# Two top-k retrievals: candidate pairs summed on GpSimd instead of VectorE, ten row steps and several orders moved

## The chip, the cores and the metric

One Trainium2 chip, of which the kernel uses one core. The metric is the device time of one execution in microseconds. Engines are called as in the profile: PE (TensorE), PEld (its weight loads), DVE (VectorE), ACT (ScalarE), POOL (GpSimd) and SP (SyncE).

## The reference

One step of a hybrid decoder layer over 1024 prompt tokens and 64 sample tokens, model width 1024: dilated sliding-window attention, a gated width-3 convolution, a merge, a layer norm, then PEER, a product-key expert layer, and a second norm. What matters here is the retrieval in PEER, for each token and each of 8 heads:

```python
s1 = einsum('chk,nk->chn', qy[..., :half], k1)      # 128 scores, side 0
s2 = einsum('chk,nk->chn', qy[..., half:], k2)      # 128 scores, side 1
v1, i1 = lax.top_k(s1, 16)
v2, i2 = lax.top_k(s2, 16)
cand = v1[..., :, None] + v2[..., None, :]           # pairs of candidates
cid = i1[..., :, None] * 128 + i2[..., None, :]
sc, pos = lax.top_k(cand, 16)
eid = take_along_axis(cid, pos)                      # 16 of 16384 experts
g = softmax(sc)
out = sum_k (g * gelu(x . u[eid])) * v[eid]
```

## The kernel before

Tokens are in two halves: EARLY (A, 512 tokens, four tiles of 128) and LATE (B, 576 tokens, five tiles, the last with 64). The stages follow one another, each a block that all engines leave together: attention; convolution gates, branches, norm and retrieval of A; the same four stages of B; `build_gates`; `experts`; the second norm.

The two halves use different expert paths. For B, `build_gates` makes a dense gate matrix and `experts` multiplies all 16384 experts on PE. For A, each of 512 (token tile, choice) pairs is a *row*: POOL fetches the chosen rows of u and v by indirect DMA (`fetch_rows`), DVE takes a dot product (`dot_row`), ACT a Gelu per eight rows (`row_gelus`), and DVE adds the weighted v row (`weigh_row`). One `row_step(y)` is the dot of row y and the weighted sum of row y-16. The 528 row steps are laid by hand into the stages of B: 60 into the convolution, 16 into the branches, none into norm, retrieval and gates, 452 into `experts`. Inside a stage, `spread(y0, total, weights)` lays them on slots; the convolution has 40 slots (8 output tiles, five units each: unit 1 carries the taps, unit 2 the gated product) with equal weights. u rows and v rows have rings of four buffers, so POOL fetches row y+4 when `dotted` says that row y is done.

In a retrieval, for each head and side x: PE makes queries (`split3`, three matmuls for full precision), ACT copies their high part (`q_hi`), POOL subtracts to get the remainder (`q_lo`), PE makes scores, ACT copies them (`s_copied`). POOL also makes the weight remainder of the next head (`split_w`, `w_lo`). DVE ranks each side (`top16`: max, match_replace, max, two max_index), adds candidate pairs (`cand`, 16x4 + 12x4 of them per token), converts indices to f32 (`ixf`), chooses the best 16 pairs and splits their positions (`pos_ready`). POOL then turns positions into a distance to 0..15 (L1534, L1921), ACT makes one-hots, POOL multiplies by the indices and halves the width (`looked_up`), and DVE's `finish` reduces it, one head later. B's retrieval is rolled into loops over pairs of heads. The order of every engine's work is written out by hand; POOL's loop of B is `queries(i)`, then `look_up(i-2)`. In A, PE and ACT also do the sample tokens' cached attention in between.

Of the kernel before, what the change touches and what calls it, by code (L numbers as in the profile page):

```python
# [17 lines left out]
P = 128  # L18
# [682 lines left out]
def conv_gates(nc, io, k, half, y0, rows):  # L701
# [5 lines left out]
    at_row = spread(y0, rows, [1] * NQ)  # L707
# [574 lines left out]
def retrieve_early(nc, io, k):  # L1282
# [14 lines left out]
    with ExitStack() as c:  # L1297
# [46 lines left out]
        s_ready, s_copied = sem("qA_s_ready"), sem("qA_s_copied")  # L1344
        topped, e_ready, e_done = sem("toppedA"), sem("e_readyA"), sem("e_doneA")
# [172 lines left out]
        def _(pool):  # L1518
# [9 lines left out]

            def distances(h):
# [21 lines left out]
            for i in range(HEADS + 1):  # L1551
                if i >= 2:
                    distances(i - 2)
                for x in range(2):
                    if i < HEADS:
                        query(i, x)
                        split_w(i + 1, x)
                    if i >= 2:
                        look_up(i - 2, x)
            distances(HEADS - 1)  # L1560
# [4 lines left out]
        def _(dve):  # L1565
# [24 lines left out]
            def pairs(h):  # L1590
                p = h % 2
                for row, rows, cols, at in ((0, A, K, 0), (A, K - A, B, A * K)):
                    m = dve.tensor_tensor(cand[:, :, at:at + rows * cols].rearrange("p t (a b) -> p t a b", b=cols),
                                          v[:, 0, :, row:row + rows].unsqueeze(3).to_broadcast([P, TL, rows, cols]),
                                          v[:, 1, :, :cols].unsqueeze(2).to_broadcast([P, TL, rows, cols]), ALU.add)
                m.then_inc(topped, 1)
                dve.tensor_copy(ixf[:, p], ix[:])
                dve.drain()
# [171 lines left out]
def retrieve(nc, io, k, half):  # L1770
# [5 lines left out]
    with ExitStack() as c:  # L1776
# [39 lines left out]
        topped = sem("topped")  # L1816
# [5 lines left out]
        block = c.enter_context(nc.Block())  # L1822
# [27 lines left out]
        def _(act):  # L1850
# [9 lines left out]
            def queries(h, more=True):  # L1860
# [9 lines left out]

            def scores(h, p):
                act.wait_ge(topped, h + 1)
                for x in range(2):
                    act.wait_ge(s_ready, h * 2 + (x + 3))
                    m = act.activation(s1[:, p, x, :FULL], ps[:, 3].rearrange("p (t n) -> p t n", n=P), ACT.Copy)
                    if half is LATE:
                        m = act.activation(s1[:NS, p, x, FULL], ps[:NS, 4, :P], ACT.Copy)
                    m.then_inc(s_copied, 1)
# [14 lines left out]
            for x in range(2):  # L1893
                split_w(0, x)
            over_heads(act, lambda i, p, more: (queries(i, more), scores(i, p)),
                       lambda i, p: (exp(i, p), one_hot(i)))

        @block.gpsimd
        def _(pool):
# [16 lines left out]

            def look_up(h, p):
# [14 lines left out]
            pool.wait_ge(consts, 48)  # L1932
            for x in range(2):
                split_w(0, x)
            over_heads(pool, lambda i, p, more: queries(i, more), look_up)

        @block.vector
        def _(dve):
# [21 lines left out]
            def top(h, p):  # L1960
                dve.wait_ge(s_copied, h * 2 + 3)
                dve.memset(tick[:], 0.0)
                for x in range(2):
                    top16(lambda t, n: s1[:n, p, x, t], lambda t, n: wk[:n, x, t],
                          lambda t, n, a: v[:n, x, t, a:a + 8], lambda t, n, a: ix[:n, x, t, a:a + 8])
                for row, rows, cols, at in ((0, A, K, 0), (A, K - A, B, A * K)):
                    m = dve.tensor_tensor(cand[:, :, at:at + rows * cols].rearrange("p t (a b) -> p t a b", b=cols),
                                          v[:, 0, :, row:row + rows].unsqueeze(3).to_broadcast([P, TL, rows, cols]),
                                          v[:, 1, :, :cols].unsqueeze(2).to_broadcast([P, TL, rows, cols]), ALU.add)
# [35 lines left out]

            top(0, 0)
            with dve.Fori(0, (HEADS - 2) // 2) as q:
                for p in range(2):
                    top(q * 2 + (p + 1), 1 - p)
                    finish(q * 2 + p, p)  # L2010
            top(HEADS - 1, 1)
            finish(HEADS - 2, 0)
            finish(HEADS - 1, 1)

        @block.tensor
        def _(pe):
# [7 lines left out]
            with pe.Fori(0, HEADS) as h:  # L2024
# [8 lines left out]
                for x in range(2):  # L2033
# [499 lines left out]
def program(nc, io, phases=99):  # L2533
# [12 lines left out]
    with ExitStack() as c:  # L2546
# [67 lines left out]
        with ExitStack() as ret:  # L2614
# [3 lines left out]
            phase(retrieve, LATE)  # L2618
# [3 lines left out]
        phase(experts, y0[3])  # L2622
# [88 lines left out]
```

## Time and profile before

| | us |
|---|---|
| median of three runs | 4020.37 (4016.74 to 4021.99) |
| the profiled execution | 4025.86 |
| its span, first to last instruction | 4024.1 |
| retrieval of A | about 1080 to 1326 |
| convolution of B | 1332 to 1617 |
| retrieval of B | 1798 to 2066 |
| experts | 2241 to 3972 |

Busy over the whole span: PE 3616.4 us (90%), DVE 2998.9 (75%), POOL 1790.2 (44%), ACT 1229.7 (31%). The mean granted clock of PE is 0.946 of full speed. In a timeline row the first number is the start in us from the span's start, the second the duration; a bracket at the end is the idle time of that engine before it and who ended it.

### The profile page before, as it was taken

To read this page: it belongs to the slowest core of one execution; us is meant where nothing else is said; L and a number is where in the kernel's file an instruction comes from. 1 tells how busy PE (TensorE), PEld (TensorE's weight loads), DVE (VectorE), ACT (ScalarE), POOL (GpSimd) and SP (SyncE) were. 2 spreads that over 40 slices of the span, in tenths; PEclk is the share of its full clock that TensorE was granted. 3 is DMA by queue.
4 is the path that set the end of the run, shared out by engine and by line. 5 is a ranking of instruction groups with operands and counts; after the bars stand their busy time and mean duration, and the time that the engine had idled before them with its cause. 6 is when DMAs were issued, how large, how long until landed. Compare 5 with 4: busy or idle time off the path is not lost. (4 is left out here: it accounts for less than half of the span.)

```text
span 4024.1 us, 64681 instructions
## 1 busy us (share of the span) xinstructions
PE 3616.4 (90%) x25095; PEld 3404.7 (85%) x25095; DVE 2998.9 (75%) x5917; ACT 1229.7 (31%) x2041; POOL 1790.2 (44%) x1364
## 2 busy tenths in 40 slices
PE   8999997998787799878549999999999999999998
PEld 8999997886675799858538899999999999999986
DVE  3434433434489588757979799999989999899997
ACT  2313313222254222124349422222222222222221
POOL 0000000000166355316769466666666666666661
PEclk9999998999898899989769999999999999999999
DMA  4122121897464587931018899999999999999996
GB/s 137 41 77 72 29 78 36 327 377 222 152 225 148 196 316 297 334 116 54 16 55 239 290 386 385 368 387 387 379 361 369 388 379 375 369 380 384 377 362 227
DMA packets 473387, 1015.56 MB, mean 252 GB/s; under 512 B 49552, under 2 KB 247824, under 8 KB 471176
## 3 DMA queue, kind: packets, MB, share of 16 engines
q0 software_dynamic: 149264, 543.49, 35.7%
q1 hardware_dynamic: 322600, 463.64, 33.2%
q8 instruction: 193, 3.16, 0.3%
q10 hardware_dynamic: 1232, 4.46, 0.3%
q14 instruction: 98, 0.80, 0.1%
HBM read 938.38 MB, written 126.82 MB: 265 GB/s over the span
## 5 line engine op out<-in xcount | busy, mean ns | idle before, releaser
L607 POOL DMA_INDIRECT u_row<-in_peer_u_dram,eid x512 | 731.1, 1428 | 622.2 <-DVE dots L625 496.0
L81 PE MATMUL e_ps<-coef_h,v_h 128*128 128x288 f32 x2048 | 617.7, 302 | 56.9 <-DVE v_l L2328 43.9
L613 POOL DMA_INDIRECT v_row<-in_peer_v_dram,eid x512 | 581.5, 1136 | 187.3 <-issue 155.0
L642 DVE SCALAR_TENSOR_TENSOR f_row<-v_row,g_coef,f_row 128x1024 f32<-128x1024 f32 x508 | 652.7, 1285 | 3.9 <-DMA v_row<-in_peer_v_dram,eid 2.8
L625 DVE CUSTOM_DVE_ANT_0 u_row<-u_row,h_row 128x1024 f32<-128x1024 f32 x512 | 621.8, 1215 | 5.1 <-DMA h_row<-s_h 2.8
L81 PE MATMUL e_ps<-tokens_Bh,u_h 128*128 128x288 f32 x2048 | 607.7, 297 | 8.0 <-DVE u_l L2322 7.2
L83 PE MATMUL e_ps<-coef_h,v_l 128*128 128x288 f32 x2048 | 614.0, 300 | 0.0
L82 PE MATMUL e_ps<-coef_l,v_h 128*128 128x288 f32 x2048 | 613.3, 299 | 0.0
L82 PE MATMUL e_ps<-tokens_Bl,u_h 128*128 128x288 f32 x2048 | 606.6, 296 | 0.0
L83 PE MATMUL e_ps<-tokens_Bh,u_l 128*128 128x288 f32 x2048 | 603.7, 295 | 0.0
L81 PEld LDWEIGHTS e_ps<-coef_h,v_h 128*128 128x128 f32 x2048 | 394.7, 193 | 66.4 <-DVE v_l L2328 50.4
L82 PEld LDWEIGHTS e_ps<-coef_l,v_h 128*128 128x128 f32 x2048 | 394.6, 193 | 0.0
L83 PEld LDWEIGHTS e_ps<-coef_h,v_l 128*128 128x128 f32 x2048 | 394.0, 192 | 0.0
L81 PEld LDWEIGHTS e_ps<-tokens_Bh,u_h 128*128 128x128 f32 x2048 | 385.9, 188 | 9.3 <-DVE u_l L2322 8.3
L83 PEld LDWEIGHTS e_ps<-tokens_Bh,u_l 128*128 128x128 f32 x2048 | 386.6, 189 | 0.0
L82 PEld LDWEIGHTS e_ps<-tokens_Bl,u_h 128*128 128x128 f32 x2048 | 386.2, 189 | 0.0
L276 POOL DMA_DIRECT2D s_att<-attS x4 | 2.3, 586 | 685.8 <-ACT attS L336 685.8
L2281 ACT ACTIVATE v_h<-v_raw 128x512 fp32r<-128x512 f32 x256 | 158.6, 627 | 419.5 <-PE e_ps L83 298.9
L2266 ACT ACTIVATE x_tmp<-e_ps 128x576 f32<-128x576 f32 x128 | 83.2, 650 | 419.7 <-PE e_ps L83 400.7
L81 PE MATMUL c_psB<-tokens_Bh,c_whB 128*128 128x288 f32 x640 | 192.6, 301 | 20.5 <-DVE c_wlB L834 20.5
L82 PE MATMUL c_psB<-tokens_Bl,c_whB 128*128 128x288 f32 x640 | 191.4, 299 | 0.0
L83 PE MATMUL c_psB<-tokens_Bh,c_wlB 128*128 128x288 f32 x640 | 190.4, 298 | 0.0
(431 smaller groups left out, 8365.0 us busy)
## 6 DMA issues: line engine op xcount, KB each, us to landing
u_raw<-in_peer_uT_dram SPq DMA_DIRECT2D x128, 512.0 KB
v_raw<-in_peer_vQ_dram SPq DMA_DIRECT2D x256, 256.0 KB
s_g<-gate_block SPq DMA_DIRECT2D x9, 4096.0 KB, 16.1
x_gate<-s_g SPq DMA_DIRECT2D x64, 576.0 KB
out_o_kv_sample_dram<-in_cache_kv_w_dram SPq DMA_DIRECT2D x32, 1016.0 KB, 8.6
c_rawA<-in_conv_tiles_dram SPq DMA_DIRECT2D x40, 512.0 KB, 6.4
c_rawB<-in_conv_tiles_dram SPq DMA_DIRECT2D x40, 512.0 KB
w_raw<-in_w_in_dram SPq DMA_DIRECT2D x96, 192.0 KB
```

The source lines that it names most:

```text
L81: pe.matmul(out, lh, rh, start=first, stop=False)
L82: pe.matmul(out, lh, rl, start=False, stop=False)
L83: return pe.matmul(out, ll, rh, start=False, stop=last)
L276: pool.dma_start(io["s_att"][s][:, :SEQ], attS[:]).then_inc(att_out, 16)
L607: pool.indirect_dma_start(k["u_row"][:, r % RING], None, io["peer_u"][0], bass.IndirectOffsetOnAxis(ap=k["eid"][:, r:r + 1], axis=0)).then ...
L613: pool.indirect_dma_start(k["v_row"][:, v % RING], None, io["peer_v"][0], bass.IndirectOffsetOnAxis(ap=k["eid"][:, v:v + 1], axis=0)).then ...
L625: dve.tensor_tensor_reduce(row, row, k["h_row"][:, t % 2], 1.0, 0.0, ALU.mult, ALU.add, k["dots"][:, s % 2, x:x + 1]).then_inc(k["dotted"], 1)
L642: dve.scalar_tensor_tensor(out=f, in0=row, scalar=coef, in1=f, op0=ALU.mult, op1=ALU.add).then_inc(k["weighed"], 1)
L2266: act.activation(tmp[:, e % 2].rearrange("p (y n) -> p y n", y=2), ps[:, 2 * (e % 2):2 * (e % 2) + 2, :CW], ACT.Gelu).then_inc(gelu_done, 1)
L2281: act.activation(vh[:, n % VS], vraw[:, n % VR], ACT.Copy).then_inc(v_hi, 1)
```

## The change

In both retrievals the candidate sums and the index conversion go from DVE to POOL (`pairs`), and DVE runs `finish` of the preceding head between ranking and choosing (`choose`). In B's retrieval PE takes queries and scores side by side (query 0, scores 0, query 1, scores 1), ACT copies each side's scores behind its query (`sides`), and DVE ranks a side when its scores are copied. Six row steps come ahead of B's first ranking, four ahead of its last `finish`; their fetches are in POOL's queue of that block, and `experts` begins ten steps later. The 60 steps of the convolution get weights 2, 0, 1, 2, 2 over the five units. B's retrieval block omits the drain of POOL at its end.

```diff
 def conv_gates(nc, io, k, half, y0, rows):
-    at_row = spread(y0, rows, [1] * NQ)
+    at_row = spread(y0, rows, [2, 0, 1, 2, 2] * KD)
...
 def retrieve_early(nc, io, k):
@@ POOL
+            def pairs(h):
+                pool.wait_ge(topped, h + 1)
+                for row, rows, cols, at in ((0, A, K, 0), (A, K - A, B, A * K)):
+                    pool.tensor_tensor(cand[...], v[:, 0, ...], v[:, 1, ...], ALU.add)
+                pool.tensor_copy(ixf[:, h % 2], ix[:])
+                pool.drain()
+                pool.sem_inc(paired, 1)
...
                     if i >= 2:
                         look_up(i - 2, x)
+                if i >= 1:
+                    pairs(i - 1)
...
@@ DVE
-            def pairs(h):
+            def choose(h):
-                for row, rows, cols, at in ((0, A, K, 0), (A, K - A, B, A * K)):
-                    m = dve.tensor_tensor(cand[...], v[:, 0, ...], v[:, 1, ...], ALU.add)
-                m.then_inc(topped, 1)
-                dve.tensor_copy(ixf[:, p], ix[:])
-                dve.drain()
+                dve.wait_ge(paired, h + 1)
+                dve.memset(tick[:], 0.0)
                 top16(...)
...
                 if i >= 1:
                     rank(i - 1, 1)
-                    pairs(i - 1)
+                    dve.sem_inc(topped, 1)
                 if i >= 2:
                     finish(i - 2)
+                if i >= 1:
+                    choose(i - 1)
...
 def retrieve(nc, io, k, half, y0, first_rows, last_rows):
-        block = c.enter_context(nc.Block())
+        block = c.enter_context(nc.Block(no_gpsimd_drain=True))
...
@@ ACT, in sides(h, p), for each x
                     if more:
                         split_w(h + 1, x)
-            def scores(h, p):
-                act.wait_ge(topped, h + 1)
-                for x in range(2):
+                    act.wait_ge(topped, h + 1)
                     act.wait_ge(s_ready, h * 2 + (x + 3))
                     act.activation(s1[:, p, x, :FULL], ps[:, 3].rearrange(...), ACT.Copy)
                     act.activation(s1[:NS, p, x, FULL], ps[:NS, 4, :P], ACT.Copy).then_inc(s_copied, 1)
+            row_gelus(act, k, y0, y0 + first_rows)
+            over_heads(act, sides, lambda i, p: (exp(i, p), one_hot(i)))
+            row_gelus(act, k, y0 + first_rows, y0 + first_rows + last_rows)
...
@@ POOL; pairs as above, waits topped >= h + 3
+            for r in range(y0 + RING, y0 + RING + first_rows // 2):
+                fetch_rows(pool, k, io, r)
             for x in range(2):
                 split_w(0, x)
-            over_heads(pool, lambda i, p, more: queries(i, more), look_up)
+            for r in range(y0 + RING + first_rows // 2, y0 + RING + first_rows):
+                fetch_rows(pool, k, io, r)
+            queries(0)
+            queries(1)
+            pairs(0, 0)
+            with pool.Fori(0, (HEADS - 4) // 2) as q:
+                for p in range(2):
+                    queries(q * 2 + (p + 2))
+                    look_up(q * 2 + p, p)
+                    pairs(q * 2 + (p + 1), 1 - p)
+            for i in (HEADS - 2, HEADS - 1):
+                queries(i, i < HEADS - 1)
+                look_up(i - 2, i % 2)
+                pairs(i - 1, 1 - i % 2)
+            look_up(HEADS - 2, 0)
+            pairs(HEADS - 1, 1)
+            look_up(HEADS - 1, 1)
+            for r in range(y0 + RING + first_rows, y0 + RING + first_rows + last_rows):
+                fetch_rows(pool, k, io, r)
...
@@ DVE
-                dve.wait_ge(s_copied, h * 2 + 3)
                 for x in range(2):
+                    dve.wait_ge(s_copied, h * 2 + (x + 2))
                     top16(...)
-                for row, rows, cols, at in ((0, A, K, 0), (A, K - A, B, A * K)):
-                    m = dve.tensor_tensor(cand[...], v[:, 0, ...], v[:, 1, ...], ALU.add)
-                m.then_inc(topped, 1)
-                dve.tensor_copy(ixf[:, p], ix[:])
-                dve.drain()
+                dve.sem_inc(topped, 1)
...
+            for y in range(y0, y0 + first_rows):
+                row_step(dve, k, y)
             top(0, 0)
+            choose(0, 0)
             with dve.Fori(0, (HEADS - 2) // 2) as q:
                 for p in range(2):
                     top(q * 2 + (p + 1), 1 - p)
                     finish(q * 2 + p, p)
+                    choose(q * 2 + (p + 1), 1 - p)
             top(HEADS - 1, 1)
             finish(HEADS - 2, 0)
+            choose(HEADS - 1, 1)
+            for y in range(y0 + first_rows, y0 + first_rows + last_rows):
+                row_step(dve, k, y)
             finish(HEADS - 1, 1)
...
@@ PE
                         m.then_inc(q_ready, 1)
-                for x in range(2):
                     pe.wait_ge(q_lo, h * (2 * NC) + ((x + 2) * NC))
                     pe.wait_ge(s_copied, h * 2 + (x + 1))
...
 def program(nc, io, phases=99):
-            phase(retrieve, LATE)
+            phase(retrieve, LATE, y0[3], 6, 4)
...
-        phase(experts, y0[3])
+        phase(experts, y0[3] + 10)
```

## Rows read from the trace of the kernel before

**Rows 1.** Busy time in two stages: second retrieval, expert stage.

```profile
1828.80:2049.90 221.10, 125.61 (x879) 122.80 (x878) 203.20 (x1098) 80.85 (x134) 146.33 (x82) 0.79 0.09 26
...
2300.00:3900.00 1600.00, 1548.82 (x11435) 1538.92 (x11434) 1518.46 (x2030) 416.32 (x647) 1082.30 (x842) 0.98 0.99 378
```

**Rows 2.** Timeline of POOL, first retrieval: start, us, instruction, idle before.

```profile
1120.96 2.54 POOL L1523 TENSOR_TENSOR q_wlA<-q_rawA,q_whA 128x1024 fp32r<-128x1024 f32 x1
...
1184.21 3.81 POOL L1534 TENSOR_TENSOR q_hotA<-pos_parts_fA,count16A 128x1024 f32<-128x1024 f32 x2 [7.92 <-DVE selA L1628]
...
1205.01 1.29 POOL L1543 TENSOR_TENSOR q_hotA<-q_hotA 128x512 f32<-128x512 f32 x1
1209.61 3.83 POOL L1534 TENSOR_TENSOR q_hotA<-pos_parts_fA,count16A 128x1024 f32<-128x1024 f32 x2 [3.32 <-DVE selA L1628]
...
1289.89 3.81 POOL L1534 TENSOR_TENSOR q_hotA<-pos_parts_fA,count16A 128x1024 f32<-128x1024 f32 x2 [8.48 <-DVE selA L1628]
...
1300.42 1.25 POOL L1543 TENSOR_TENSOR q_hotA<-q_hotA 128x512 f32<-128x512 f32 x1
1311.61 3.81 POOL L1534 TENSOR_TENSOR q_hotA<-pos_parts_fA,count16A 128x1024 f32<-128x1024 f32 x2 [9.94 <-DVE selA L1628]
```

**Rows 3.** Timeline of DVE, first retrieval: one head's choosing, first and last.

```profile
1302.44 0.81 DVE L1578 MAX8 bestA<-candA 128x8 f32<-128x112 f32 x4
...
1309.36 0.23 DVE L1614 TENSOR_TENSOR pos_parts_fA<-best_pos_fA,row_firstA 128x64 f32<-128x64 f32 x1
```

**Rows 4.** Timeline of POOL, second retrieval: one look-up and the next.

```profile
1915.86 4.71 POOL L1921 TENSOR_TENSOR q_hotB<-pos_parts_fB,count16B 128x1280 f32<-128x1280 f32 x2 [4.89 <-DVEq L2003]
...
1928.76 1.56 POOL L1929 TENSOR_TENSOR q_hotB<-q_hotB 128x640 f32<-128x640 f32 x1
...
1943.27 4.68 POOL L1921 TENSOR_TENSOR q_hotB<-pos_parts_fB,count16B 128x1280 f32<-128x1280 f32 x2 [4.84 <-DVEq L2003]
```

**Rows 5.** Timeline of DVE, second retrieval: ranks, pair sums, choosing.

```profile
1916.37 1.06 DVE L1954 MAX8 top_vB<-scoresB 128x8 f32<-128x128 f32 x5
...
1929.72 1.86 DVE L1967 TENSOR_TENSOR candB<-top_vB 128x320 f32<-128x320 f32 x2
...
1932.42 0.97 DVE L1954 MAX8 bestB<-candB 128x8 f32<-128x112 f32 x5
...
1940.48 0.24 DVE L1988 TENSOR_TENSOR pos_parts_fB<-best_pos_fB,row_firstB 128x80 f32<-128x80 f32 x1
```

**Rows 6.** Waits of PE: convolution 1340 to 1612, experts 2300 to 3900.

```profile
PE c_psB L81 <- DVE c_wlB L834: 17.9, 10, 3.4
...
PE e_ps L81 <- DVE v_l L2328: 43.9, 14, 8.5
```

**Rows 7.** Groups by shape, POOL's query remainders, first and second retrieval.

```profile
L1527 POOL TENSOR_TENSOR q_lA<-q_fullA,q_hA 128x512 fp32r<-128x512 f32 x16 | 20.6, 1285 | 46.7 <-ACT q_hA L1422 46.7
...
L1912 POOL TENSOR_TENSOR q_lB<-q_fullB,q_hB 128x288 fp32r<-128x288 f32 x32 | 26.9, 854 | 28.3 <-ACT q_hB L1867 28.3
```

**Rows 8.** DVE's pair sums, first retrieval: ns min/median/max.

```profile
L1593 DVE TENSOR_TENSOR candA<-top_vA x16: 346/788/2521, 1120.0 to 1301.9; 128x256 f32<-128x256 f32 x8, 128x192 f32<-128x192 f32 x8
```

**Rows 9.** Timelines at the second retrieval's start: PE, ACT, DVE.

```profile
1808.00 0.60 PE L81 MATMUL q_psB<-tokens_Bh,q_whB 128*128 128x288 f32 x1 [6.48 <-POOL q_wlB L1906]
...
1813.46 0.41 ACT L1866 ACTIVATE q_fullB<-q_psB 128x288 f32<-128x288 f32 x1 [6.54 <-PE q_psB L83]
...
1816.66 0.41 ACT L1866 ACTIVATE q_fullB<-q_psB 128x288 f32<-128x288 f32 x1 [2.49 <-PE q_psB L83]
...
1827.91 0.60 ACT L1875 ACTIVATE scoresB<-q_psB 128x512 f32<-128x512 f32 x1 [2.59 <-PE q_psB L83]
...
1828.80 0.30 DVE L1954 MAX8 top_vB<-scoresB 128x8 f32<-128x128 f32 x1 [26.41 <-ACT scoresB L1877]
```

**Rows 10.** Timelines: PE after the second retrieval; POOL's fetches, DVE idle.

```profile
2066.19 3.52 PE L2137 MATMUL g_ps<-ident,sel 128*128 128x128 f32 x15 [74.65 <-PEq L1776]
...
1331.26 0.94 POOL L607 DMA_INDIRECT u_row<-in_peer_u_dram,eid  x1 [0.30 <-issue]
```

More of the change, by code:

```diff
@@ L1344, in retrieve_early @@
         s_ready, s_copied = sem("qA_s_ready"), sem("qA_s_copied")
+        paired = sem("pairedA")
         topped, e_ready, e_done = sem("toppedA"), sem("e_readyA"), sem("e_doneA")
@@ L1527, in query @@
                 pool.tensor_tensor(ql[:, x], qf[:], qh[:, x].bitcast(F32), ALU.subtract).then_inc(q_lo, 1)
+            def pairs(h):
+                pool.wait_ge(topped, h + 1)
+                for row, rows, cols, at in ((0, A, K, 0), (A, K - A, B, A * K)):
+                    pool.tensor_tensor(cand[:, :, at:at + rows * cols].rearrange("p t (a b) -> p t a b", b=cols),
+                                       v[:, 0, :, row:row + rows].unsqueeze(3).to_broadcast([P, TL, rows, cols]),
+                                       v[:, 1, :, :cols].unsqueeze(2).to_broadcast([P, TL, rows, cols]), ALU.add)
+                pool.tensor_copy(ixf[:, h % 2], ix[:])
+                pool.drain()
+                pool.sem_inc(paired, 1)
             def distances(h):
@@ L1767, in _, with retrieve @@
                     turn_out(i - 1)
-def retrieve(nc, io, k, half):
+def retrieve(nc, io, k, half, y0, first_rows, last_rows):
     K = TOPK
@@ L1815, in retrieve @@
         s_copied = sem("q_s_copied")
-        topped = sem("topped")
+        topped, paired = sem("topped"), sem("paired")
         e_ready, e_done = sem("e_ready"), sem("e_done")
@@ L1858, in split_w, with sides @@
                 act.activation(wh[:, x], raw[:, x], ACT.Copy).then_inc(w_hi, 1)
-            def queries(h, more=True):
+            def sides(h, p, more=True):
                 for x in range(2):
@@ L1869, in queries @@
                         split_w(h + 1, x)
-            def scores(h, p):
-                act.wait_ge(topped, h + 1)
-                for x in range(2):
+                    act.wait_ge(topped, h + 1)
                     act.wait_ge(s_ready, h * 2 + (x + 3))
[L1875 to L1878, printed above, removed]
+                    act.activation(s1[:, p, x, :FULL], ps[:, 3].rearrange("p (t n) -> p t n", n=P), ACT.Copy)
+                    act.activation(s1[:NS, p, x, FULL], ps[:NS, 4, :P], ACT.Copy).then_inc(s_copied, 1)
             def exp(h, p):
@@ L1894, in _ @@
                 split_w(0, x)
-            over_heads(act, lambda i, p, more: (queries(i, more), scores(i, p)),
+            row_gelus(act, k, y0, y0 + first_rows)
+            over_heads(act, sides,
                        lambda i, p: (exp(i, p), one_hot(i)))
+            row_gelus(act, k, y0 + first_rows, y0 + first_rows + last_rows)
         @block.gpsimd
@@ L1915, in queries, with pairs @@
                         split_w(h + 1, x)
+            def pairs(h, p):
+                pool.wait_ge(topped, h + 3)
+                for row, rows, cols, at in ((0, A, K, 0), (A, K - A, B, A * K)):
+                    pool.tensor_tensor(cand[:, :, at:at + rows * cols].rearrange("p t (a b) -> p t a b", b=cols),
+                                       v[:, 0, :, row:row + rows].unsqueeze(3).to_broadcast([P, TL, rows, cols]),
+                                       v[:, 1, :, :cols].unsqueeze(2).to_broadcast([P, TL, rows, cols]), ALU.add)
+                pool.tensor_copy(ixf[:, p], ix[:])
+                pool.drain()
+                pool.sem_inc(paired, 1)
             def look_up(h, p):
@@ L1960, in top, with choose @@
             def top(h, p):
-                dve.wait_ge(s_copied, h * 2 + 3)
-                dve.memset(tick[:], 0.0)
                 for x in range(2):
+                    dve.wait_ge(s_copied, h * 2 + (x + 2))
+                    dve.memset(tick[:], 0.0)
                     top16(lambda t, n: s1[:n, p, x, t], lambda t, n: wk[:n, x, t],
                           lambda t, n, a: v[:n, x, t, a:a + 8], lambda t, n, a: ix[:n, x, t, a:a + 8])
-                for row, rows, cols, at in ((0, A, K, 0), (A, K - A, B, A * K)):
-                    m = dve.tensor_tensor(cand[:, :, at:at + rows * cols].rearrange("p t (a b) -> p t a b", b=cols),
-                                          v[:, 0, :, row:row + rows].unsqueeze(3).to_broadcast([P, TL, rows, cols]),
-                                          v[:, 1, :, :cols].unsqueeze(2).to_broadcast([P, TL, rows, cols]), ALU.add)
-                m.then_inc(topped, 1)
-                dve.tensor_copy(ixf[:, p], ix[:])
-                dve.drain()
+                dve.sem_inc(topped, 1)
+            def choose(h, p):
+                dve.wait_ge(paired, h + 1)
+                dve.memset(tick[:], 0.0)
                 top16(lambda t, n: cand[:n, t], lambda t, n: rest[:n, t],
```

3 lines of the change are left out of this document (removed).

## The prediction

> **What bounds the kernel now.** I read the page first. Its 40 slices show three kinds of stretch: projections with TensorE (PE) near 9, two short stretches near the middle where PE falls and DVE stays high (the two retrievals), and the long expert stage with PE and DVE both at 9. The stage windows put numbers on it [rows 1]: in 1,600 us of the expert stage PE is busy 1,549 and DVE 1,518, at clock 0.98. In the second retrieval DVE is busy 203 of 221 us, GpSimd (POOL) only 146, PE 126. So the retrievals look DVE bound and POOL looks like spare room, which is what tempts one to move the pair sums. But a busy share hides order, so I read the timelines of POOL and DVE over one head.
>
> In the first retrieval POOL begins the distances of a head when DVE has finished the one before it, at 1184.2, and ends that head's look-up at 1206.3: 22.1 us later. It then waits 3.3 us and starts the next at 1209.6 [rows 2]. DVE meanwhile ranks (about 13 us), pairs, chooses (7.15 us undisturbed, 1302.44 to 1309.6) [rows 3] and finishes. Most of the 22.1 us thus lies under ranking *and* choosing. The second retrieval has the same shape: look-up 1915.9 to 1930.3, 14.5 us; then the queries' remainders and weight splits until 1938.4, 8.2 us; then a wait to 1943.3, so a period of 27.4 us [rows 4]. DVE's choosing there takes 8.3 us [rows 5].
>
> Around them, PE waits 17.9 us (10 times) for DVE's weight remainders in the second convolution, and 43.9 us (14 times) for v_l in the expert stage [rows 6].
>
> **What moves, and what it costs: the pair sums.** POOL has no row for these shapes. Its two subtractions at 512 and 288 elements take 1.29 and 0.85 us, so 0.30 us plus 1.9 ns an element [rows 7]. Sums of 256 and 192 and the conversion of 128 come to 0.79+0.67+0.55 = 2.0 us, in the second retrieval (320, 240, 160) 2.3; with drain and two semaphore hops I take 2.3 and 2.6. Bounds: not below DVE's best (two sums at 0.35 each [rows 8] and the cast, 1.1 us with hops); above, 4 us if the broadcast operands or the uint32 read cost POOL as much again.
> DVE's own sums take 0.35 to 2.5 us, median 0.79 [rows 8]; the long ones stand beside a POOL operation and end with it. The Trainium skill, page "SBUF — State Buffer", section "Who interferes with whom", says a DVE instruction with two SBUF inputs and a GpSimd instruction that reads SBUF exclude each other for a whole instruction. The trace agrees (2.5 against 0.35 us), and by that rule the move would also win back DVE's blocked time, 10 to 20 us over both stages, if DVE set the period; this is the third rival's mechanism.
>
> **What the move does to the order.** This decides. On POOL, the pairs of head i-1 are queued *behind* the look-up of head i-2, and DVE's choosing of i-1 now waits for them; the distances of i-1 wait for that choosing. A cycle closes: look-up, pairs, choosing, next look-up. Choosing no longer covers the look-up.
> First retrieval: the first choosing starts after POOL's weight split ends (1120.96+2.54 = 1123.5 [rows 2]) plus 2.3, and ends 7.15 later at 1133.0. Then seven periods. Five are 22.1+2.3+7.15 = 31.6 us; one lacks two splits of 2.5 us, 26.6; the last has only distances and look-ups, 1289.89 to 1301.7 = 11.8 [rows 2], so 21.3. Sum 206, last distances at 1338.7 against 1311.6 [rows 2]: **+27 us**. With pairs at 1.1 or 4 us per head: +18 to +41.
>
> Second retrieval: here the regrouping adds a second stretch. Until now PE ran both queries of a head before any scores. Now it runs query 0, scores 0, query 1, scores 1, in order, and scores 0 needs POOL's remainder of query 0. That remainder is queued behind the preceding pairs. So after the pairs end: two remainders 1.6; scores 0, 2.6 (ACT waits that long for them at 1827.9); query 1 in two chunks of 3.2 (1813.46 to 1816.66); ACT 0.7; ACT's weight copy 1.1 and POOL's split 2.4. That is 14.8. PE has by then idled some 10 us, and after an idle of 6.5 us its first chunk took 5.4 instead of 3.2 us (1808.0 to 1813.46, at the 1.2 GHz level) [rows 9]; the scores' 2.6 already hold part of that, so I add 1.0: 15.8 us where 8.2 stood. DVE's choosing (8.3) no longer covers it. Period: 15.8+14.5+2.6 = 32.9 us against 27.4. DVE alone would need 13.35 (ranks, 1916.37 to 1929.72 [rows 5]) +0.7+2.6+8.3 = 25.
>
> Its start: DVE gets 6 row steps after 1802.4, at about 2.4 us each, into an idle of 26.4 us before 1828.8 [rows 9]: hidden. Their fetches are 12 indirect DMAs on POOL at 0.94+0.3 us each when alone [rows 10], more beside DVE. Three pairs of them stand ahead of the first split and each waits for a row step, so the split starts at about 1812 instead of 1805.5; the other three delay the first query remainder to about 1825. Side 0 is ranked from 1830, side 1 from 1839.5 to 1846.2 (before: both done 1842.5). Then POOL has the whole of queries(1) before pairs(0): scores, both queries of head 1 and two splits in series, to 1859. Pairs(0) ends at 1861.6, the first choosing at 1869.9. Pairs(1) ends at 1895.7 (its query 0 isn't precomputed yet), four more at 32.9, to 2027.3; one without a split, 30.5, to 2057.8. Choosing 8.3, look-up 14.5, pairs 2.6, choosing 8.3 bring 2091.5. Four row steps (9.6 us) lie under the last look-up (14.2), free. It ends 2105.7; POOL then issues 8 indirect DMAs, 8 x 1.25 = 10 us, and PE's first transpose of the next block waits for nothing but the block's end: 2066.2 before [rows 10], 2115.7 now. **+49 us**, of which the last fetches are some 8. Bounds +35 (pairs 1.1, no clock loss) to +70. The omitted GpSimd drain is costed at nothing: before has no DMA of POOL's in flight there. ACT gets one Gelu, under PE's first query; with table loads of 1.3 us nothing waits for it.
>
> **What the rest gives.** Convolution: no row step after the taps, one after the gating, two elsewhere. DVE's slot then is at most 1.2+2x2.4 = 6.0 us or the taps plus split, against PE's 6.4 to 6.7. Of the 17.9 us most go; rounding (60 steps on 56 weights) leaves some: **-14** (0 to -18). Expert stage: ten steps fewer of 452, 24 us of DVE work. PE waits once per group of about 107 us, at the first v_l, when DVE comes late out of the coefficient part; per group 0.6 step goes, of it 0.3 before that wait, 0.7 us, 16 times: **-11** (0 to -25, all of it if DVE set the whole stage; its 82 us idle [rows 1] say no). The first convolution has no row steps, so its weights change nothing.
>
> **Sum.** 27+49-14-11 = +51. The profiled execution took 4025.9 us (span 4024.1), 5.5 above the median shown; so 4077 on its own scale, 4071 on that of the median.
>
> **Rivals.**
> (a) *Only the cross-head cycle binds.* The new order in the second retrieval costs POOL nothing, say because remainders overlap scores better than I read. DVE and the look-up cycle then give 25.3 instead of 27.4, seven times -15; start and tail +17; with +27-25 that is +4: 4024. For it: POOL's 8.2 us of queries alone would fit under choosing. Against: query 1 stands behind scores 0 in PE's own program.
> (b) *Pairs are dear on POOL and the gains stay out.* 4 us per head: 15 x 1.5 = +23, and convolution and experts give half, +12: 4106. For it: four-dimensional broadcasts and uint32. The Trainium skill, page "GPSIMD Engine Reference", section "4.1 Engine selection", puts two-input elementwise work at about twice the Vector engine's time; the sum by it would be about mine, not this.
> (c) *Faster.* DVE sets both periods. The mechanism: DVE loses its sums and their blocked time, about 2.8 us in 16 heads, -45; plus -25 elsewhere, plus 11 for start and tail: 3961. It decides only if POOL ends a look-up before DVE ends its ranks, at 13 us after the distances begin. The rows show 22.1 and 14.5, so it fails by 9 us in the first retrieval and by little in the second.
> (d) *The pair move changes nothing*, as its waits fit in DVE's slack: row steps and order alone, -25+11 = 4006. The same point decides as in (c).
>
> **Chances.** Forecast 0.72, (a) 0.08, (b) 0.13, (c) 0.04, (d) 0.03. The range takes the forecast with its bounds and most of (a) and (b): combining +18..+41, +35..+70, 0..-18 and 0..-25 without all ends at once gives 4032 to 4104; that is also the likeliest's own range. A measurement of this kernel tells 0.2% (8 us) from no change. Faster: (c), (d) and a bit: 0.07. Same: the centre of (a): 0.04. Slower: 0.89.
>
> **What would show it.** In the first retrieval the starts of POOL's distances should be 31 to 32 us apart (before 25.4), with POOL waiting about 7 us for pos_parts each time, and DVE idle 6 to 9 us a head before the reduction of q_hotA. In the second, about 33 us apart, POOL waiting for q_hB between remainders, PE's query 1 beginning after the pairs, DVE idle about 15 us before the first choosing. The last fetches stand between the last look-up and PE's transposes. PE's wait for c_wlB falls below 6 us, that for v_l to some 33. Wrong if DVE's idle time in the retrievals doesn't grow, or the pairs take under 1 us, or PE's queries run ahead of scores.

## The result

The changed kernel takes 4080.65 us (median of four runs, 4078.24 to 4085.95), the kernel before 4018.55 us beside it on the same chip: ratio 1.0156 [1.0138, 1.0173], 62 us slower. The forecast was +51 us, 4071 in 4032 to 4104. The profiled execution took 4085.95 us, span 4083.8, clock 0.941, so it is compared with the span of before, 4024.1: +59.7.

I cut both spans at the same events: the first distances of the first retrieval, the first matmul of B's convolution, the first matmul of its branches, the memset of the second retrieval, PE's first transpose after it, and PE's first matmul of the last stage. In microseconds, worked out from the starts of those instructions:

| stretch | before | after | difference | forecast |
|---|---|---|---|---|
| up to the first distances (same code but for the first pairs) | 1131.2 | 1127.2 | -4.0 | 0 |
| first retrieval | 204.3 | 228.1 | +23.8 | +27 |
| second convolution | 292.8 | 273.0 | -19.8 | -14 |
| branches and mix | 170.2 | 174.3 | +4.1 | 0 |
| second retrieval | 267.7 | 330.1 | +62.4 | +49 |
| gates and experts | 1909.2 | 1903.0 | -6.2 | -11 |
| the rest | 48.7 | 48.1 | -0.6 | 0 |

The forecast counted its first distances at 1133.0, so about 2 of its +27 lie in the first line. The difference measured there, -4.0, is no effect that I can name: in all the kernels run here that stretch took between 1121.9 and 1131.2, and 1127.7 in a kernel whose code up to there is that of before. Gates and experts spread too: see below.

**The profile after.** First the timeline of POOL over one head of the first retrieval (start, us, instruction, idle before it), which answers to [rows 2]:

```profile
1189.43 3.81 POOL L1545 TENSOR_TENSOR q_hotA<-pos_parts_fA,count16A 128x1024 f32<-128x1024 f32 x2 [7.38 <-DVE pos_parts_fA L1622]
...
1204.20 1.28 POOL L1528 TENSOR_TENSOR q_lA<-q_fullA,q_hA 128x512 fp32r<-128x512 f32 x1 [1.96 <-ACT q_hA L1423]
...
1210.26 1.28 POOL L1554 TENSOR_TENSOR q_hotA<-q_hotA 128x512 f32<-128x512 f32 x1
1211.50 1.09 POOL L1533 TENSOR_TENSOR candA<-top_vA 128x256 f32<-128x256 f32 x2
1212.53 0.29 POOL L1536 CAST top_ifA<-top_iA 128x128 f32<-128x128 uint32 x1
1220.21 1.93 POOL L1545 TENSOR_TENSOR q_hotA<-pos_parts_fA,count16A 128x1024 f32<-128x1024 f32 x1 [7.39 <-DVE pos_parts_fA L1622]
```

Read it as a ring: look-up 22.1 us (1189.43 to 1211.5), pairs 1.3, then 7.39 us idle in which DVE chooses, and the next distances 30.8 us after the last. Before, the two rows that the prediction read show a wait of 3.3 us and a period of 25.4; over the whole stage the periods before were 24.6 to 28.4 us, long and short in turn, until the last one (21.7). Experiment 3 comes back to that.

The same in the second retrieval, over one period, against [rows 4]:

```profile
1928.77 4.70 POOL L1938 TENSOR_TENSOR q_hotB<-pos_parts_fB,count16B 128x1280 f32<-128x1280 f32 x2
...
1943.06 1.28 POOL L1927 TENSOR_TENSOR candB<-top_vB 128x320 f32<-128x320 f32 x2
1944.28 0.32 POOL L1930 CAST top_ifB<-top_iB 128x160 f32<-128x160 uint32 x1
1945.11 1.54 POOL L1919 TENSOR_TENSOR q_lB<-q_fullB,q_hB 128x288 fp32r<-128x288 f32 x2 [0.52 <-issue]
1946.61 2.36 POOL L1913 TENSOR_TENSOR q_wlB<-q_rawB,q_whB 128x1024 fp32r<-128x1024 f32 x1
1956.15 0.80 POOL L1919 TENSOR_TENSOR q_lB<-q_fullB,q_hB 128x288 fp32r<-128x288 f32 x1 [7.18 <-ACT q_hB L1877]
1959.27 0.80 POOL L1919 TENSOR_TENSOR q_lB<-q_fullB,q_hB 128x288 fp32r<-128x288 f32 x1 [2.32 <-ACT q_hB L1877]
1960.22 2.37 POOL L1913 TENSOR_TENSOR q_wlB<-q_rawB,q_whB 128x1024 fp32r<-128x1024 f32 x1
1962.55 4.70 POOL L1938 TENSOR_TENSOR q_hotB<-pos_parts_fB,count16B 128x1280 f32<-128x1280 f32 x2
```

The distances follow the last weight split with no idle time at all: here POOL's own list is the ring. Look-up 14.3, pairs 1.6, queries 17.9, of which 7.18 + 2.32 are waits for the second query, which PE began only after the first side's scores. PE's timeline over that stretch, the first side's scores and then the second side's query:

```profile
1946.78 0.47 PE L81 MATMUL q_psB<-keys_hB,q_hB 128*128 128x128 f32 x1 [9.10 <-POOL q_lB L1919]
...
1949.72 0.55 PE L81 MATMUL q_psB<-tokens_Bh,q_whB 128*128 128x288 f32 x1
1950.07 0.44 PE L82 MATMUL q_psB<-tokens_Bl,q_whB 128*128 128x288 f32 x1
...
1954.74 0.30 PE L82 MATMUL q_psB<-tokens_Bl,q_whB 128*128 128x288 f32 x1
```

After 9.1 us of idling the scores and, until 1954, the query's matmuls run at PE's lower clock level (granted clock 0.50 from 1946.8 to 1954.0, 0.44 us a matmul of the query), then at the higher one (1.00 from 1954.6 to 1956.1, 0.30 us). The granted clock over the stage is 0.73 (before 0.79). The stage's window, with the columns of [rows 1], and the waits of PE in the convolution and in the expert stage [rows 6]:

```profile
1837.78:2108.60 270.82, 153.29 (x942) 149.64 (x941) 187.22 (x1091) 84.12 (x141) 160.59 (x109) 0.73 0.08 23
```

```profile
PE c_psB L81 <- DVE c_wlB L834: 5.6, 4, 2.6
```

```profile
PE e_ps L81 <- DVE v_l L2369: 27.7, 13, 8.7
PE e_ps L81 <- DVE u_l L2363: 15.4, 4, 4.3
```

DVE was busy for 203 of 221 us there before and is now for 187 of 271. It got its relief, 16 us, and waits 66 us more. The next rows are the timeline of all engines at the retrieval's end:

```profile
2108.67 6.57 POOL L1938 TENSOR_TENSOR q_hotB<-pos_parts_fB,count16B 128x1280 f32<-128x1280 f32 x2 [8.88 <-DVE pos_parts_fB L2023]
...
2122.53 3.88 DVE L642 SCALAR_TENSOR_TENSOR f_row<-v_row,g_coef,f_row 128x1024 f32<-128x1024 f32 x1
...
2125.48 2.32 POOL L1946 TENSOR_TENSOR q_hotB<-q_hotB 128x640 f32<-128x640 f32 x1
...
2127.95 1.79 POOL L607 DMA_INDIRECT u_row<-in_peer_u_dram,eid  x1 [0.15 <-issue]
2128.81 1.27 DVE L642 SCALAR_TENSOR_TENSOR f_row<-v_row,g_coef,f_row 128x1024 f32<-128x1024 f32 x1
...
2131.47 0.81 DVE L2037 TENSOR_REDUCE sel<-q_hotB 128x80 f32<-128x640 f32 x1
...
2132.75 3.52 PE L2178 MATMUL g_ps<-ident,sel 128*128 128x128 f32 x15 [71.70 <-PEq L1786]
...
2137.57 0.95 POOL L613 DMA_INDIRECT v_row<-in_peer_v_dram,eid  x1 [0.30 <-issue]
2138.86 4.36 POOL L2156 TENSOR_TENSOR hot<-hot,selT 128x512 f32<-128x512 f32 x4 [0.34 <-DVE hot L2167]
```

The last look-up, beside DVE's row steps, takes 19.1 us (2108.67 to 2127.8), the others 14.3. The row steps suffer too: an accumulation takes 3.88 us beside POOL and 1.27 once POOL only fetches, so that they end at 2130.1, 2.3 us after the look-up, and finishing follows them. PE does not wait for the eight fetches, which go on until 2138.5: it starts 0.5 us after DVE's last instruction, so here not all engines leave the block together. That the block omits POOL's drain may be the reason; no run here has the drain back. POOL's first work in the next block follows its last fetch after 0.34 us.

### The profile page after: what moved, and what is told of

It reads as the page before. It is cut to its first block and busy times, and to the rows that moved or that the text cites. A ratio compares the mean times of both kernels' runs of the same rounds, so it can differ in the third digit from the quotient of the medians.

```text
span 4083.8 us, 64726 instructions
## 1 busy us (share of the span) xinstructions
PE 3632.3 (89%) x25095; PEld 3412.6 (84%) x25095; DVE 2971.2 (73%) x5893; ACT 1231.1 (30%) x2042; POOL 1825.5 (45%) x1412
## 5 line engine op out<-in xcount | busy, mean ns | idle before, releaser
L642 DVE SCALAR_TENSOR_TENSOR f_row<-v_row,g_coef,f_row 128x1024 f32<-128x1024 f32 x508 | 662.6, 1304 | 2.9 <-DMA v_row<-in_peer_v_dram,eid 2.1
L81 PE MATMUL e_ps<-coef_h,v_h 128*128 128x288 f32 x2048 | 613.8, 300 | 44.4 <-DVE v_l L2369 27.7
L81 PE MATMUL e_ps<-tokens_Bh,u_h 128*128 128x288 f32 x2048 | 609.3, 297 | 15.4 <-DVE u_l L2363 15.4
L2363 DVE TENSOR_TENSOR u_l<-u_raw,u_h 128x1024 fp32r<-128x1024 f32 x128 | 155.8, 1218 | 48.5 <-ACT u_h L2301 45.2
```

Source lines behind the costliest of these rows:

```text
L81: pe.matmul(out, lh, rh, start=first, stop=False)
L642: dve.scalar_tensor_tensor(out=f, in0=row, scalar=coef, in1=f, op0=ALU.mult, op1=ALU.add).then_inc(k["weighed"], 1)
L2363: dve.tensor_tensor(ul[:, e % 2], uraw[:, e % 2], uh[:, e % 2].bitcast(F32), ALU.subtract).then_inc(u_lo, 1)
```

## The experiments

All times are medians of four runs or more, beside runs of the kernel before on the same chip (4017 to 4021 us). A difference against the changed kernel is taken against its 4080.65, across chips.

**1. The weights of the row steps alone** (`conv_weights`), on the kernel before:

```
-    at_row = spread(y0, rows, [1] * NQ)
+    at_row = spread(y0, rows, [2, 0, 1, 2, 2] * KD)
```

> The kernel before with the new weights of the row steps in the convolution and nothing else. Theory: the 19.8 us by which the second convolution got shorter come from the weights alone (fewer late weight remainders), so about 3999 (3996 to 4003), convolution 273 us from first to last stage boundary, waits for c_wlB under 6 us. Rival: part of the 19.8 us came because the longer retrieval ahead left the transfers more time; then the gain is 8 to 14 us, 4005 to 4011, and waits of PE on raw weights' transfers or on remainders stay above 9 us.

Measured: 3999.49 us, ratio 0.9949 [0.9931, 0.9967], 17.6 us faster. Convolution 271.8 us (before 292.8), the wait for c_wlB from 20.5 us over the whole stretch to 4.1; branches and mix 173.5 (170.2). So the gain belongs to the weights, and so do the 3 to 4 us that the branches give back: the kernels with the new weights have 172.6 to 175.7 there, those without them 170.0 and 170.2. The waits explain 16 of the 21 us; PE's busy time fell by 4.8 us more (263.8 to 259.0), at a granted clock of 0.98 instead of 0.97.

**2. The first retrieval's change alone** (`first_alone`), on the kernel before: `retrieve_early` as in the changed kernel.

> The kernel before with only the first retrieval changed (pair sums and index conversion on GpSimd, choosing after finishing). Theory: the cycle look-up, pairs, choosing costs by itself: distances 30 to 31 us apart, +24 us, 4043 (4038 to 4048). Rival: the 4.6 us by which the changed kernel was already ahead at the start of this stage are no chance but belong to it, then +20, 4038. Second rival, that the stage's delay is hidden by transfers further on: 4019.

Measured: 4051.1 us, ratio 1.0079 [1.0061, 1.0097], +34, where 24 was expected (19 to 29 by its range). The first retrieval is no more than expected: distances up to 30.6 us apart, the stage +20.3. But the second retrieval, whose code this kernel doesn't touch, took 275.0 instead of 267.7 us. More of that under experiment 8. The two profiles differ by 26.7 us only, since the profiled execution of before was 9 us above the median that it is compared with here; the stages therefore don't locate the last 7 us.

**3. Where the pairs stand in the first retrieval** (`first_between`), on the changed kernel, two edits:

```
                     if i >= 2:
                         look_up(i - 2, x)
-                if i >= 1:
-                    pairs(i - 1)
+                    if i >= 1 and x == 0:
+                        pairs(i - 1)
...
+                if i >= 1:
+                    choose(i - 1)
                 if i >= 2:
                     finish(i - 2)
-                if i >= 1:
-                    choose(i - 1)
```

> The changed kernel, but in the first retrieval GpSimd does the pairs between the two look-ups of the preceding head, and DVE chooses before it finishes that head. The sums stay on GpSimd. Theory (it is the place in the queue, not GpSimd's price): topped comes 14.6 us after the distances begin, where GpSimd waits 2 us anyway, so choosing overlaps the second look-up again and the period falls from 30.8 to about 25; minus 26 us (20 to 40), about 4055. Rival (GpSimd's slower sums cost the time): the period stays near 30 and the time at 4075 to 4081.

Measured: 4041.48 us, 39 us less than the changed kernel. The timeline of POOL, a head of that kernel:

```profile
1198.64 3.82 POOL L1545 TENSOR_TENSOR q_hotA<-pos_parts_fA,count16A 128x1024 f32<-128x1024 f32 x2 [3.31 <-DVE selA L1636]
...
1211.65 1.09 POOL L1533 TENSOR_TENSOR candA<-top_vA 128x256 f32<-128x256 f32 x2
...
1219.26 1.28 POOL L1554 TENSOR_TENSOR q_hotA<-q_hotA 128x512 f32<-128x512 f32 x1
1223.86 1.93 POOL L1545 TENSOR_TENSOR q_hotA<-pos_parts_fA,count16A 128x1024 f32<-128x1024 f32 x1 [3.32 <-DVE selA L1636]
```

The sums cost the same 1.09 us, but 9.1 us earlier in the ring, and DVE chooses beside the second look-up. The period is 25.2, and the stage takes 196.8 us: 31 less than in the changed kernel and 7.5 less than with the sums on DVE. Of the rest of the 44 us between the two spans, 5.1 lie ahead of the first distances and 4.0 in gates and experts, whose spread is of that size.

The 7.5 us are no chance: the five kernels with both edits take 196.3 to 198.1 us in this stage, the two with the code of before 204.3 and 205.0. Their order on DVE is that of before, so what differs is who sums. DVE's timeline before, in a short and in a long period:

```profile
1143.89 0.69 DVE L1593 TENSOR_TENSOR candA<-top_vA 128x256 f32<-128x256 f32 x2
...
1168.87 3.79 DVE L1593 TENSOR_TENSOR candA<-top_vA 128x256 f32<-128x256 f32 x2
1172.58 2.38 DVE L1597 CAST top_ifA<-top_iA 128x128 f32<-128x128 uint32 x1
```

In the long ones (28.4 us) POOL's subtraction, weight split and multiplication run beside them, and sums and conversion take 6.1 us instead of 0.8; in the short ones (24.6 to 25.7) they hardly meet. With the sums on POOL the second to fifth period take 25.0 to 25.4.

**4. One of those two edits** (`first_finish_first`): the pairs between the look-ups, DVE's order as in the changed kernel.

> The changed kernel with the pairs between the two look-ups in the first retrieval, but DVE still finishes the preceding head before it chooses. It parts first_between into its two edits. Theory (the cycle is closed twice: on GpSimd by the place of the pairs and on DVE by finishing, which waits for the second look-up): the period stays at 30 to 32 us, 4076 to 4086. Rival (the place in GpSimd's queue alone is what costs): 25 to 26 us, 4041 to 4050.

Measured: 4083.13 us; distances 30.7 to 31.0 us apart, POOL waiting 8.7 us for pos_parts. No gain: finishing waits for the second look-up, and choosing stands behind it on DVE. The ring had two links, and cutting this one alone does nothing; the other alone (choosing first, pairs behind the look-up) was not run.

**5. The grouping in the second retrieval** (`second_ungrouped`), on the changed kernel: PE and ACT do both queries before both scores.

```
                         m.then_inc(q_ready, 1)
+                for x in range(2):
                     pe.wait_ge(q_lo, h * (2 * NC) + ((x + 2) * NC))
...
```

> The changed kernel, but in the second retrieval PE and ACT do both queries of a head before both scores, as before. Pairs stay on GpSimd behind the look-up, rows stay. Theory (the grouping by side puts the second query behind the pairs): GpSimd's stretch from pairs to distances falls from 17.2 to 8 to 9 us and lies beside choosing, so the period is 25 us instead of 33 and the time 4081-50 = 4031 (4022 to 4040). Rival (the pairs in GpSimd's queue are what costs there, as in the first retrieval): the period falls by no more than 2 us, 4066 to 4081.

Measured: 4021.43 us, 59 us less than the changed kernel, just under the range expected, and 1.0012 [1.0003, 1.0022] of before. On POOL's timeline the queries' work stands together again:

```profile
1918.94 4.71 POOL L1941 TENSOR_TENSOR q_hotB<-pos_parts_fB,count16B 128x1280 f32<-128x1280 f32 x2 [1.99 <-DVE pos_parts_fB L2026]
...
1933.30 1.28 POOL L1930 TENSOR_TENSOR candB<-top_vB 128x320 f32<-128x320 f32 x2
1934.53 0.31 POOL L1933 CAST top_ifB<-top_iB 128x160 f32<-128x160 uint32 x1
...
1940.42 2.36 POOL L1916 TENSOR_TENSOR q_wlB<-q_rawB,q_whB 128x1024 fp32r<-128x1024 f32 x1
1944.77 2.37 POOL L1941 TENSOR_TENSOR q_hotB<-pos_parts_fB,count16B 128x1280 f32<-128x1280 f32 x1 [1.99 <-DVE pos_parts_fB L2026]
```

From the cast to the last split 7.9 us where 17.9 stood, then 1.99 us of waiting for DVE: the period is 25.8, less than before's 27.4. So once the queries are ungrouped, the pairs on POOL and DVE's new order are together a gain in this stage; no run parts these two. From the first to the last distances it takes 178.2 us; before 187.4, changed 213.1. Its start, from the memset to the first distances, takes 72.6 (before 64.1, changed 93.0). The stage as a whole takes 274.9 against before's 267.7: start and end, each some 8 us longer, carry the row steps (experiment 7).

**6. The sums back on DVE, the grouping kept** (`second_dve_pairs`), on the changed kernel; in the second retrieval DVE also chooses before it finishes, as before.

> The changed kernel, but in the second retrieval DVE does the pair sums and the conversion again, and chooses before it finishes; the grouping by side and the rows stay. Theory (the grouping costs by itself: GpSimd's stretch of queries of 17 us and the look-up of 14.2 us are in series on GpSimd whoever sums): period 31 to 32 us where 33 stood, 4070 (4062 to 4078). Rival (the grouping costs only because the query remainders are queued behind the pairs): period 27 to 28, 4040 (4032 to 4050).

Measured: 4072.58 us. POOL's timeline, one period of 31.0 us:

```profile
1959.20 4.69 POOL L1928 TENSOR_TENSOR q_hotB<-pos_parts_fB,count16B 128x1280 f32<-128x1280 f32 x2
...
1973.52 1.54 POOL L1919 TENSOR_TENSOR q_lB<-q_fullB,q_hB 128x288 fp32r<-128x288 f32 x2
...
1983.81 0.80 POOL L1919 TENSOR_TENSOR q_lB<-q_fullB,q_hB 128x288 fp32r<-128x288 f32 x1 [6.43 <-ACT q_hB L1877]
...
1990.20 2.39 POOL L1928 TENSOR_TENSOR q_hotB<-pos_parts_fB,count16B 128x1280 f32<-128x1280 f32 x1
```

The stretch of 16.7 us and the look-up of 14.3 stand in series on POOL, whoever sums. The grouping costs by itself; the pairs, with DVE's new order, add 8 us on top.

**7. No row steps in the second retrieval** (`no_rows`): `phase(retrieve, LATE, y0[3], 0, 0)` and `phase(experts, y0[3])`. **The sums done twice** (`pairs_twice`): the loop over both sums a second time behind a drain, the same values again.

> The changed kernel with no row step inside the second retrieval; the expert stage starts ten steps earlier in the list, as before. Theory (the steps are paid on GpSimd's side): without the six fetch pairs ahead the first query remainder comes about 7 us sooner; without DVE's row steps the last look-up takes 14.2 instead of 19.1 us; without the eight last fetches PE's transposes follow the look-up some 1.5 us after it instead of 4.9; that is minus 15 us in the retrieval, plus 6 to 8 in the expert stage: 4073 (4066 to 4080). Rival (steps in DVE's idle time are free and save 7 to 11 us of the expert stage): 4088 to 4092.

> The changed kernel with GpSimd's two pair sums done twice per head in both retrievals, which writes the same values again. Theory (they are a link of both cycles): each head's period grows by the 1.1 us (first) and 1.3 us (second) that they take, 7 periods each and the start of the second, so plus 18 us, 4099 (4092 to 4104). Rival (they lie in slack or only their place counts): 4079 to 4085.

Measured without row steps: 4065.35 us, 15 less and just under the range expected; the retrieval takes 307.2 instead of 330.1 us. Its start is 79.4 instead of 93.0, its end, from the second half of the last distances to PE, 13.9 instead of 20.8, as before. I had expected 7 us at the start; they are 13.6. POOL's timeline in the changed kernel shows where they begin:

```profile
1808.40 1.28 POOL L607 DMA_INDIRECT u_row<-in_peer_u_dram,eid  x1 [5.87 <-DVE dots L625]
...
1817.11 0.95 POOL L613 DMA_INDIRECT v_row<-in_peer_v_dram,eid  x1 [0.31 <-issue]
1818.08 5.80 POOL L1913 TENSOR_TENSOR q_wlB<-q_rawB,q_whB 128x1024 fp32r<-128x1024 f32 x2
```

The fetches put the first split, and so PE's first query, back by 8.4 us (18.1 against 9.7 after the memset). The second three pairs of fetches stand ahead of the query's remainders; in all the first pair sums end 12.1 us later (69.9 against 57.8 us after the memset). Over all profiles, gates and experts take 1905.8 to 1910.8 us in the seven kernels without steps in the retrieval (mean 1909.0) and 1898.7 to 1903.0 in the seven with them (mean 1900.1): the steps bring 9 us back there and cost 23.

Measured with the sums twice: 4093.48 us, +12.8. The first retrieval grows by 6.0 and the second by 8.4, where seven periods and a start at 1.1 and 1.3 us would have made 8 and 10. The added work is paid at about three quarters, far from the rival's 4 us at most, short of the 18 expected.

**8. What adds up** (`best_no_rows`, `best_rows`): the edits of experiments 3 and 5 together, without and with the ten row steps in the second retrieval.

> The changed kernel with pairs between the look-ups and choosing before finishing in the first retrieval, both queries before both scores in the second, and no row steps there. Theory: the three are in stages of their own and add up: 4081-39-59-8 = 3975 (3965 to 3985), the first retrieval 7 us shorter than in the kernel before, the second 5 to 8 us shorter. Rival (what they give is one and the same wait, or a transfer behind them takes it back): 3995 or more, no better than the new weights alone (3999.5).

> The kernel of best_no_rows with the ten row steps in the second retrieval again (six ahead, four behind). Theory (steps there cost 8.5 us at its start and 7 at its end and give back 7 to 10 in the expert stage; the two turns of DVE's loop that began 5.2 and 4.4 us late in best_no_rows don't come, as they didn't with the steps in second_ungrouped): 3992-7.5+15.5-10 = 3990 (3985 to 3996). Rival (the steps are a loss here too, and the late turns come from the first retrieval's edit): 3996 to 4002.

Measured: 3992.29 us, ratio 0.993 [0.9914, 0.9947], and 3991.31, ratio 0.9931 [0.9914, 0.9948]. Both beat before. They lie below the 3999.5 of the new weights alone too, but on another chip and with intervals that overlap that kernel's. The first misses its 3975. The first retrieval took 198.1 and 196.9 us, as it should. The second took 267.4 without the steps, where 256 was due: two of its periods are 30.1 and 29.3 us instead of 25.9. On DVE's timeline two turns of the loop begin late with nothing to wait for. These are the rows of the first of them; in the second (1941.80) the same instructions stand idle for 3.0 and 1.4 us:

```profile
1886.48 0.06 DVE L2003 MEMSET q_tickB<- 128x1 f32 x1 [3.69 <-issue]
...
1889.07 0.09 DVE L1995 MATCH_VALUE_LOAD scores_restB<-top_vB,scoresB 128x8 f32 x1 [1.53 <-issue]
```

The scores that the turn ranks had been copied by 1881.6, 4.9 us before. The profile of `first_alone` has such gaps in the same stage (3.3 and 1.7, 3.1 and 1.6 us), in line with its 7 us there, and so has `no_rows` (twice 3.0 and 1.3 us, partly in idle time). The seven kernels with steps ahead of the loop have none, but neither have before and `conv_weights`, without steps.

**9. Is it where the code lies?** (`best_pad12`, `best_pad32`): `best_no_rows` with memsets of one element and drains on DVE ahead of the first head.

```
+            for y in range(12):
+                dve.memset(tick[:], 0.0)
+                dve.drain()
             top(0, 0)
```

> The kernel of best_no_rows with 12 one-element memsets and drains (24 more instructions) on DVE ahead of the first head of the second retrieval, in idle time. It moves DVE's code and changes nothing else. Theory (DVE's late loop turns, with no wait behind them, depend on where the loop's code lies): the late turns vanish or change in number and place; if they vanish 3984 to 3986, if not 3992. Rival (they come from something on the chip beside DVE's own code, such as the work of other engines at that time): the same two late turns, third and fifth period, 3992.

> As the kernel with 12 of them, with 32 memsets and drains (64 more instructions). Theory of placement: late turns that differ from those of best_no_rows, or none: 3984 to 3992. Rival: the same two late turns at the third and fifth period, 3992.

Measured: 3982.6 us with 12, ratio 0.9908 [0.9891, 0.9926], the fastest of all and clear of the new weights alone; 3991.89 with 32. With 12 the late turns are gone and the retrieval takes 256.3 us. With 32 they are there again, in the same two periods (29.6 and 28.2 us), idle for 4.4 us in the first and 3.0 in the second. So 24 instructions that compute nothing take 10 us off, and 64 don't. That fits the place of DVE's code; but the added instructions also shift times (the first distances come 61.9 us after the memset with 12 of them, 64.0 with 32, 64.2 without), and no run parts the two. The cause is not shown.

## Why the prediction was right

The direction, the mechanism and the range held: two rings closed, as it said. Most of its signs came: distances 30.8 and 32 to 34 us apart, POOL's waits of 7.4 us for pos_parts, DVE idle 6.3 to 9.8 us a head before it finishes in the first retrieval, POOL waiting between the remainders, c_wlB under 6 us. Three did not come as written. The last fetches stand in POOL's queue where it said, but PE did not wait for them; DVE idled 20 us before the first choosing instead of 15; and v_l fell further than said. And "before 25.4" was the period of one head of a stage that had 24.6 to 28.4. The median lies 10 us above the forecast, as the sum of terms that were off both ways:

- *First retrieval, +27: measured +23.8, and +19 to +24 in the other kernels with this edit.* The ring held: 22.1 + 1.3 + 7.15 = 30.6, measured 30.8. The pairs were mis-sized: 2.3 us forecast, 1.33 measured. One sum takes 0.51 to 0.62 us; the line that I drew through POOL's larger operations (0.30 us and 1.9 ns an element) [rows 7] was too high below 300 elements. The bound of 1.1 us was the nearer one. Against that, the period with fewer splits took 28.4 us, not 26.6: POOL waited 4.3 us there for the second query.
- *Second retrieval, +49: measured +62.4.* The whole of this miss is in its start. From the first to the last distances the forecast has 213 us (1878.6 to 2091.5) and the trace 213.1, from there to PE 24.2 against 24.1. But the first distances come 93.0 us after the memset, not 80. The row steps were costed as "hidden" beside DVE's idle time, and the queue that pays is POOL's: its first split starts at 15.5 us and takes 5.8 beside DVE instead of 4.7, the first pairs end at 69.9 instead of 63. And the third head's queries, between those pairs and the first look-up, take 23.1 us instead of 17; they take 21.6 in `no_rows`, so most of this part was mis-sized whatever the steps do. Experiment 7 prices the steps at 13.6 us of the start. The two good numbers hold errors that cancel. In the period the pairs took 1.6 instead of 2.6 us and the queries 16.4 to 17.9 instead of 15.8: the lower clock costs PE more than the 1.0 us given to it. In the tail PE did not wait for the last fetches (10 us in the forecast); the look-up beside the row steps, costed as free, took 4.8 us more, DVE came 2.3 us late behind it, and its finishing and the way to PE, 2.6 us, had no term.
- *Convolution, -14: -19.8, and -17.6 for the whole program alone.* The wait fell as forecast. The 4.8 us less of busy time and the 4 us that the branches give back were missing.
- *Experts, -11: -6.2 in this pair of profiles, -9 over seven profiles each.* The wait for v_l fell from 43.9 to 27.7 us, below the 33 forecast; that for u_l, which I had not looked at, rose from 7.2 to 15.4 us over the whole stage and took half of it back.

Rival (a), that the grouping costs nothing, is refuted by `second_ungrouped` (59 us). Rival (b), dear pairs, is refuted by the 1.3 and 1.6 us. Rival (d), that the move of the pairs changes nothing, falls with `first_alone`. Rival (c), the faster one, named a real gain and its mechanism, DVE's blocked sums: with the pairs between the look-ups the first retrieval is 7.5 us shorter than before, and ungrouped the second has periods of 25.8 us instead of 27.4. It failed here for the reason given: POOL ends a look-up after DVE ends its ranks, so what stands behind the look-up decides.

At the retrieval's end POOL and DVE slowed each other: beside DVE's steps POOL's distances took 6.57 instead of 4.7 us, and beside POOL's look-up a DVE accumulation took 3.88 instead of 1.27. The Trainium skill, page "SBUF — State Buffer", section "Who interferes with whom", says that a DVE instruction with two SBUF inputs and a GpSimd instruction that reads SBUF exclude each other; these rows agree. The prediction weighed that rule for the gain alone, and not for the row steps.

## What to carry to other kernels

When work moves to an engine with idle time, draw the ring of waits through that engine's own list first: what it stands behind, who waits for it, and what used to run beside it. Here the same sums, 1.3 us a head, cost 24 us behind the look-up and gained 7 between its halves, once the waiting engine's order was turned too. Look at several periods of a loop, not at one: the head that was read here was a short one, and the long ones held the gain. Idle time of the engine that computes says nothing of the queue that fetches for it.

## What the runs showed of the hardware

- Turns of DVE's loop began 3.0 to 4.4 us late with no wait behind them, in one case in a stage whose code did not change (267.7 to 275.0 us). With 24 added instructions ahead of the loop they were gone (3992.3 to 3982.6 us), with 64 not. A difference of under 10 us between two of these kernels can be this.
- POOL added two operands with broadcast patterns of 192 or 256 elements (a partition) in 0.51 to 0.62 us and converted 128 uint32 values in 0.29 us. DVE, undisturbed, took 0.35 to 0.43 us for the same sums, and up to 2.5 beside POOL.
- PE began the next block 0.5 us after DVE's last instruction, while POOL still had 5.8 us of fetches to issue.
